# Two layers of a hybrid diffusion backbone on one core: another order at an FFN edge, at the start and at the end of attention

## What is computed

```python
x = x + mod[2] * rms_norm(y, mix_post_g[l])
h = modulate(rms_norm(x, ffn_pre_g[l]), mod[3], mod[4])
x = x + mod[5] * rms_norm(conv_ffn(h, ffn_w_in[l], ffn_conv_w[l], ffn_w_out[l]), ffn_post_g[l])
```

## Time and profile before

| | us |
|---|---|
| runs of the kernel | 1669.77, 1673.02, 1673.84 (median 1673.02) |
| the profiled execution's own time | 1669.0 |
| its span | 1667.3 |
| busy in the span: PE, DVE, ACT, POOL | 1607.5, 1024.0, 551.7, 54.6 |
| chain that ended last: PE, DVE, ACT, issue, POOL | 77%, 14%, 3%, 2%, 1% |

### The profile page before, as it was taken

The page is one execution under the profiler, slowest core; times in us unless marked ns, Lnnn a source line. Parts: engine busy times, 40 slices in busy tenths (PEclk is TensorE's granted clock), DMA queues, the critical chain, the costliest instruction groups (busy, mean ns, idle before and its releaser), DMA issues.

```text
span 1667.3 us, 21933 instructions
## 1 busy us (share of the span) xinstructions
PE 1607.5 (96%) x8698; PEld 1347.4 (81%) x8698; DVE 1024.0 (61%) x1457; ACT 551.7 (33%) x878; POOL 54.6 (3%) x74
## 2 busy tenths in 40 slices
PE   5999999999999999999999999898999999999998
PEld 2688887787898878888888887787778988888886
DVE  2899996659757774667626446654875644454344
ACT  3313224555633221123211225613325532232133
POOL 0500000210000000000000001100000000000001
PEclk9999999989999999999999999999999999999999
DMA  9421212334116552454323231230002233223222
GB/s 309 137 67 51 77 51 70 115 111 111 39 53 226 205 172 79 139 193 166 129 83 133 51 101 51 80 101 26 26 1 63 89 101 112 79 89 113 88 95 81
DMA packets 134009, 169.43 MB, mean 102 GB/s; under 512 B 15970, under 2 KB 92450, under 8 KB 133930
## 3 DMA queue, kind: packets, MB, share of 16 engines
q1 hardware_dynamic: 133360, 168.11, 31.5%
q10 hardware_dynamic: 570, 0.22, 0.1%
HBM read 166.17 MB, written 2.15 MB: 101 GB/s over the span
## 4 chain that ended last, share of the span: by engine, by line
PE 77%; DVE 14%; ACT 3%; issue 2%; POOL 1%; POOLq 0%; DVEq 0%; ACTq 0%
PE acc L700 39%; PE acc L755 21%; DVE conv_u L1845 7%; PE acc L726 4%; PE acc L912 2%; DVE w_lo L1570 2%; PE acc L1120 2%; PE acc L1099 2%; PE acc L813 1%; PE acc L947 1%; PE acc L1067 1%; PE acc L668 1%; DVE x L1745 1%; PE acc L925 1%; POOL y L2263 1%
## 5 line engine op out<-in xcount | busy, mean ns | idle before, releaser
L700 PE MATMUL acc<-h_hi,w_hi 128*128 128x512 f32 (+1 forms) x1424 | 414.1, 352 | 3.0 <-issue 2.4
L700 PE MATMUL acc<-h_lo,w_hi 128*128 128x512 f32 (+1 forms) x1424 | 411.1, 350 | 0.0
L700 PE MATMUL acc<-h_hi,w_lo 128*128 128x512 f32 (+1 forms) x1424 | 411.1, 350 | 0.0
L1570 DVE TENSOR_TENSOR w_lo<-raw,w_hi 128x1024 fp32r<-128x1024 f32 x183 | 219.6, 1229 | 155.6 <-ACT w_hi L1139 155.5
L700 PEld LDWEIGHTS acc<-h_hi,w_hi 128*128 128x128 f32 x1424 | 229.8, 188 | 40.6 <-issue 3.4
L1139 ACT ACTIVATE w_hi<-raw 128x1024 fp32r<-128x1024 f32 x183 | 186.5, 1055 | 225.8 <-PE acc L755 183.9
L700 PEld LDWEIGHTS acc<-h_lo,w_hi 128*128 128x128 f32 x1424 | 229.6, 188 | 37.4 <-issue 0.5
L700 PEld LDWEIGHTS acc<-h_hi,w_lo 128*128 128x128 f32 x1424 | 229.4, 188 | 37.2
L755 PE MATMUL acc<-w_hi,hid_hi 128*128 128x512 f32 x440 | 176.3, 401 | 0.0
L755 PE MATMUL acc<-w_lo,hid_hi 128*128 128x512 f32 x440 | 175.6, 399 | 0.0
L755 PE MATMUL acc<-w_hi,hid_lo 128*128 128x512 f32 x440 | 175.5, 399 | 0.0
(11 more groups left out here) (245 smaller groups left out, 2051.7 us busy)
## 6 DMA issues: line engine op xcount, KB each, us to landing
ada_w<-in_ada_w SPq DMA_DIRECT2D x88, 512.0 KB, 5.9
raw<-in_ffn_w_in SPq DMA_DIRECT2D x88, 512.0 KB, 3.6
raw<-in_ffn_w_out SPq DMA_DIRECT2D x44, 512.0 KB, 4.2
raw<-in_even_w_in SPq DMA_DIRECT2D x24, 512.0 KB, 4.5
ada<-in_ada_w SPq DMA_DIRECT2D x8, 1024.0 KB, 12.2
raw<-in_odd_w_in SPq DMA_DIRECT2D x12, 512.0 KB, 4.2
raw<-in_even_w_out SPq DMA_DIRECT2D x8, 512.0 KB, 4.5
ada_m<-in_ada_w SPq DMA_DIRECT2D x8, 512.0 KB, 4.4
```

The costliest lines, as they stand in the source:

```text
L700: last = nc.tensor.matmul(acc[:, s, m, t0:t1], w[:, slot, kk, c], x_[:, k, t0:t1], start=(k == 0 and q == 0), stop=(k == KD - 1 and q == 2))
L1570: return nc.vector.tensor_tensor(out_, in0, in1, op)
```

## The change

- **FFN edges.** POOL's part goes. DVE gates columns 512 to 1023 itself, into the scratch `ada_d`, between the sum of a tile and the wait for its root, and adds in two halves (`added`). At down02 the additions, squares and normalisations of tiles 4 and 5 come after all steps of the latent tiles and after the last granule's high and low parts. PE turns tiles 4 and 5 one after the other, after the third of the four first blocks. In every edge ACT does one Sqrt on a constant before it waits for the first half.
- **First scores.** The row sums for the keys move from behind value tile 4 to behind tile 3, score 0 from after the values to behind tile 4. ACT copies value tiles 0 to 3 when they are done, then does one Exp on a constant; tiles 4 and 5 it copies after the exponential of round 0.
- **First granule of out1.** `PAIRS` makes heads 0 and 1 its first granule, then heads 2 and 3, the pool, heads 4 and 5. Its banks change sides (near and far). The inner `step` of `token_products` becomes a function of its own, `token_step`, unchanged. Rounds 22 and 23, which have no scores to make ahead, each make two tiles of granule 0. DVE's low parts of rounds 2 and 3 move behind the loop. The first unit of the second FFN waits for the set that holds the other half of out1.

```diff
+PAIRS = {"out0": (2, 0, 1, 3), "out1": (1, 2, 0, 3)}
...
@@ tile_bank
             near, far = U[name] % 2, 1 - U[name] % 2
+            if name == "out1":
+                near, far = far, near
...
@@ token_products
-            if not freed:
+            if not freed and not begun:
                 psum_free(pe, d)
...
-                for g in range(half):
+                for g in range(1 if begun and not a else 0, half):
...
@@ ffn of PE
                         else:
+                            if l:
+                                psum_free(pe, U["up10"] + 1)
                             first_products(pe, U[f"up{l}0"], G[f"up{l}0"], h, [(256 * e, 256 * e + 256) for e in range(nt // 2)],
...
@@ first_products of in1
-                           lambda e: turn(pe, "down02", NT - 2 + e) if e < 2 else None)
+                           lambda e: [turn(pe, "down02", j) for j in (NT - 2, NT - 1)] if e == 2 else None)
...
@@ values on PE
+                if j == 3:
+                    last.then_inc(sem("v_tiles"), 1)
...
-                if j == 4:
+                if j == 3:
                     pe.wait_ge(sem("pool_taken"), 1)
                     pe.wait_ge(sem("rot_taken"), 4)
                     pe.wait_ge(sem("kdiag_ready"), 2)
...
                     last.then_inc(sem("kb_full"), 1)
+                if j == 4:
+                    pe.wait_ge(sem("v_taken"), 1)
+                    pe.wait_ge(sem("qk_ready"), 1)
+                    scores(0)
 
             u = U["att"]
             psum_free(pe, u + 1)
-            pe.wait_ge(sem("qk_ready"), 1)
...
-            scores(0)
             scores(1)
...
@@ attention rounds on PE
                 if n + 2 < N_Q * NL:
                     scores(n + 2)
+                else:
+                    pe.wait_ge(low, G["out1"] + 5)
+                    pe.wait_ge(h_ready, HEADS + 2)
+                    for j in (n % 2, n % 2 + 2):
+                        last = token_step(pe, "out1", h, 0, 0, j)
+                    if n == N_Q * NL - 1:
+                        last.then_inc(part_used, 1)
...
-            token_products(pe, "out1", h, lambda k: pe.wait_ge(h_ready, HEADS + k + 1))
+            token_products(pe, "out1", h, lambda k: pe.wait_ge(h_ready, HEADS + k - 1) if k >= 2 else pe.wait_ge(sem("pool_low"), 1),
+                           begun=True)
...
@@ edge of ACT
+                nc.scalar.activation(mark[:, 5:6], eps[:, 0:1], ACT.Sqrt)
                 act.wait_ge(y_eps, EDGES.index(name) + 1)
...
-                    act.wait_ge(x_new, q + 1)
-                    x_squares(j, NT + q, junk_x[:, :])
+                    if name != "down02" or j < NL:
+                        act.wait_ge(x_new, q + 1)
+                        x_squares(j, NT + q, junk_x[:, :])
...
                     take_high(n + 2 * half + 3)
+                    if name == "down02":
+                        for j in range(NL, NT):
+                            act.wait_ge(x_new, t.chain + j + 1)
+                            x_squares(j, NT + t.chain + j, junk_x[:, :])
...
@@ values on ACT
-            psum_full(act, u)
-            nc.scalar.activation(v1[:, 0:4, :], acc[:, u % 2, 0, :].rearrange("p (j c) -> p j c", c=256), ACT.Copy)
-            nc.scalar.activation(v1[:, 4:6, :], acc[:, u % 2, 1, 0:512].rearrange("p (j c) -> p j c", c=256), ACT.Copy
-                                 ).then_inc(set_free[u % 2], 1)
+            act.wait_ge(sem("v_tiles"), 1)
+            nc.scalar.activation(v1[:, 0:4, :], acc[:, u % 2, 0, :].rearrange("p (j c) -> p j c", c=256), ACT.Copy
+                                 ).then_inc(sem("v_taken"), 1)
+            nc.scalar.activation(mark[:, 6:7], eps[:, 0:1], ACT.Exp)
...
                 if n == 0:
+                    psum_full(act, u)
+                    nc.scalar.activation(v1[:, 4:6, :], acc[:, u % 2, 1, 0:512].rearrange("p (j c) -> p j c", c=256), ACT.Copy
+                                         ).then_inc(set_free[u % 2], 1)
                     unit_high(G["vin"] + 4)
...
@@ edge of DVE
+                def added(j):
+                    q = t.chain + j
+                    if not mixer:
+                        tile_taken(dve, name, 1, j)
+                        dve.wait_ge(x_new, q)
+                        sd.done(vt(ada_d[:, :], y[:, j, 512:1024], gates[idx][:, stream(j), 512:1024], ALU.mult))
+                    dve.wait_ge(y_root, q + 1)
+                    sd.done(nc.vector.reciprocal(yroot[:, 1, j:j + 1], yroot[:, 0, j:j + 1]))
+                    sd.wait()
...
+                    for half_, of in ((0, y[:, j, 0:512]), (1, ada_d[:, :])):
+                        x_ = x[:, j, 512 * half_:512 * half_ + 512]
+                        ins = nc.vector.scalar_tensor_tensor(x_, of, yroot[:, 1, j:j + 1], x_, ALU.mult, ALU.add)
+                    ins.then_inc(x_new, 1)
...
                     summed(name, 2, 1, j)
+                    if 1 <= j <= NL:
+                        normed(j - 1)
+                    if j >= 3:
+                        tile_low(name, j - 3)
+                    if j < NL:
+                        added(j)
+                    if j >= 2:
+                        tile_half(name, j - 2, l, comp)
...
                 if not mixer:
+                    tile_low(name, NL - 1)
+                    take_low(n + 2 * half + 3)
+                    for j in range(NL, nt):
+                        added(j)
                     nc.vector.memset(poolw[:, :, :], 0.0).then_inc(sem("poolw_zero"), 1)
-                    normed(nt - 1)
-                    tile_low(name, nt - 3)
-                take_low(n + 2 * half + 3)
+                    for j in range(NL, nt):
+                        normed(j)
...
@@ attention on DVE
-                if n == 2:
-                    unit_low(G["in1"] + 14)
-                elif n == 3:
-                    dve.wait_ge(sem("pool_high"), 1)
-                    vt(h_lo[:, 0:2, 0:LAT], ps2[:, :, 0:LAT], h_hi[:, 0:2, 0:LAT].bitcast(F32), ALU.subtract).then_inc(h_ready, 2)
...
+            dve.wait_ge(sem("pool_high"), 1)
+            vt(h_lo[:, 0:2, 0:LAT], ps2[:, :, 0:LAT], h_hi[:, 0:2, 0:LAT].bitcast(F32), ALU.subtract).then_inc(sem("pool_low"), 1)
+            unit_low(G["vin"] + 4)
             head_low(N_Q - 1)
...
@@ POOL: edge("down02") and edge("down12") removed
```

More of the change, by code:

```diff
@@ L741, in turn, with token_step, token_products @@
             last.then_inc(turned, 1)
-        def token_products(pe, name, lhs, ready, freed=None, amid=None):
+        def token_step(pe, name, lhs, a, g, j):
+            half, m_ = TOK[name].half, G[name] + a * TOK[name].half + g
+            for kk in range(2):
+                k = 2 * pair_of(name, g) + kk
+                for q, (w, x_) in enumerate(((w_hi, lhs[0]), (w_lo, lhs[0]), (w_hi, lhs[1]))):
+                    last = nc.tensor.matmul(tile_bank(name, a, j), x_[:, k, j * P:(j + 1) * P],
+                                            w[:, m_ % 4, 2 * kk:2 * kk + 2, :].rearrange("p a c -> p (a c)"),
+                                            start=(g == 0 and kk == 0 and q == 0), stop=(g == half - 1 and kk == 1 and q == 2))
+            return last
+        def token_products(pe, name, lhs, ready, freed=None, amid=None, begun=False):
             t, d, n = TOK[name], U[name], G[name]
             nt, half = t.nt, t.half
-            def step(a, g, j):
-                m_ = n + a * half + g
-                for kk in range(2):
-                    k = 2 * pair_of(name, g) + kk
-                    for q, (w, x_) in enumerate(((w_hi, lhs[0]), (w_lo, lhs[0]), (w_hi, lhs[1]))):
-                        last = nc.tensor.matmul(tile_bank(name, a, j), x_[:, k, j * P:(j + 1) * P],
-                                                w[:, m_ % 4, 2 * kk:2 * kk + 2, :].rearrange("p a c -> p (a c)"),
-                                                start=(g == 0 and kk == 0 and q == 0), stop=(g == half - 1 and kk == 1 and q == 2))
-                return last
-            if not freed:
+            if not freed and not begun:
                 psum_free(pe, d)
@@ L796, in token_products @@
                             pe.wait_ge(cols_taken, list(BESIDE).index(name) + 1)
-                        last = step(a, g, j)
+                        last = token_step(pe, name, lhs, a, g, j)
                         if g == half - 1:
@@ L1054, in _, with scores @@
             product(pe, U["kin"], G["kin"], h, always, amid=heads_45)
+            def scores(n):
+                hd, i = divmod(n, NL)
+                if n >= 2:
+                    pe.wait_ge(sem("score_exp"), n - 1)
+                for t0, t1 in SEGS[T]:
+                    last = nc.tensor.matmul(acc[:, 0, n % 2, t0:t1], inb[:, 2 + hd, i * P:(i + 1) * P],
+                                            kT[:, hd // 3, t0:t1], start=True, stop=True)
+                last.then_inc(sem("score_full"), 1)
             u, n = U["vin"], G["vin"]
@@ L1088, in _ @@
                     last.then_inc(sem("kb_full"), 1)
```

(22 more changed lines are left out.)

44 lines of the change are left out of this document (18 added, 26 removed).

## The result

The changed kernel takes 1657.41 us (median of 4 runs, 1656.99 to 1659.79). The kernel before, on the same chip, takes 1671.39 us (4 runs, 1669.67 to 1673.84). The ratio is 0.9918 with a 95% interval of 0.9904 to 0.9932: 14.0 us faster. The profiled execution of the changed kernel took 1657.77 us, its span is 1656.1 us against 1667.3 before, 11.2 us less.

What follows compares the result with a forecast made beforehand. TensorE, busy 96% of the span, bounds the kernel, so only its idle and half-clock time can be won. The terms sum to -11.35 us on 1669.0, so 1657.6; for the median, 4.0 above, 1661.6, range 1655 to 1667.

Steps and rivals of the forecast that it cites:

- rival without new cold stretches: Third unit and up10: the new waits leave the clock at full speed, 3.4 us more won, 1658.2 us; chance 0.2.
- Term 1: Edge of down02: third unit starts 4.0 us earlier, less 1.7 for a cold clock: -2.3 us.
- Term 2: Attention's start: first softmax hidden under value tile 5, rounds of 3.31 us from the start: -7.5 us.
- Term 3: Rounds 22 and 23: out1's first granule fills them, 9.7 us instead of 14.1: -4.2 us.
- Term 4: up10's first unit waits for out1's last sum: 1.7 us lost, 1.7 more for a cold clock: +3.4 us.
- Term 5: Tail, down12: the last x no longer waits 0.85 us for GpSimd, less 0.1 for the split: -0.75 us.
- The table load: Before each root: rival with ScalarE idle 1.4 us beyond the load, a drain, 1660.2 us; chance 0.03.

Runs made afterwards that it cites:

- e9: The changed kernel, nothing edited, profiled a second time: span 1656.6 us against 1656.1 in the first profile.
- e4: Changed kernel with the six tiles of down02 back in their old order, context tiles not last: 1659.23 us, ratio 0.9939 to the kernel before.
- e1: Kernel before with only the FFN edge's part of the change: 1668.45 us, ratio 0.9987.
- e7: Changed kernel with the squares and sum of out1's last tile ahead of two granules of up10: 1656.41 us, ratio 0.9910 to the kernel before.
- e2: Kernel before with only the first scores' part of the change, low parts left in rounds 2 and 3: 1666.61 us, ratio 0.9972.
- e3: Kernel before with only the part for out1's first granule, low parts moved behind the loop: 1667.41 us, ratio 0.9981.
- e5: Changed kernel without the Sqrt ahead of the edges and the Exp ahead of attention: 1662.19 us, ratio 0.9951 to the kernel before.
- e11: Changed kernel with out1's last squares and sum first, nothing further edited, profiled a second time: span 1654.4 us against 1654.9.
- e10: Changed kernel with down02's tiles in their old order, nothing further edited, profiled a second time: span 1656.5 us against 1657.4.

## Why the prediction was right

The direction and the places held, and 1657.4 lies in the range, 4.2 us below the predicted 1661.6. It is nearest to the rival without new cold stretches, 1658.2, but by luck: the third unit's stretch was there, so that rival's condition failed. Of the difference, 1.6 us are the base: I added the changes to a median of 1673.0, and the kernel before took 1671.4 beside the changed one. 2.6 us remain between the 11.35 predicted and the 14.0 of the medians. The stages explain 1.4 of them in the first profile (12.7 us in all) and none in e9 (9.7), so how near the number came is in part luck too. By the prediction's own steps:

**Term 1, edge of down02 (-2.3, measured -1.93).** Each link of the series came as listed: third unit at 1076.08, or 1074.6 less the executions' offset of 1.5 us, against 1075.0; one wait of 4.19 us against 4.5; both context tiles turned from 1064.23, or 1062.7, against 1063.0. What was mis-sized is the cold stretch: 12 matmuls at 0.43 us pitch instead of 0.23 cost 2.4 us, not 1.7. Whose merit the term is, the prediction didn't part; e4 does: VectorE's gating with the Sqrt ahead brings 2.9 us, and the new order of the tiles costs 1.0. e4's stage holds a half-clock stretch of its own behind the last granule's wait, 1.7 us of TensorE's time; with both kernels' stretches taken out, A would be 63.7 with the new order and 63.4 with the old one, an estimate, so the order would win nothing even then. The prediction also says that "its cold stretch goes too" behind the shortened first wait. It was gone in the changed kernel's two profiles, but not in those of e1 and e7, with the same wait of 1.9 us; A lost nothing by it there: 65.26, or 63.6 without the third unit's stretch, as in the changed kernel.

**Term 2, first scores (-7.5, measured -7.32).** Score 0 starts at 1150.81 with no wait. Predicted was 1151.1 on the clock of before; the key multiplication ends at 1150.18, 0.6 us ahead (0.4 was said). The value copy costs 0.69 us and pT 0.22, against 0.6 and 0.45. e2 shows what the term hid: with the low parts left in rounds 2 and 3 it was -3.1, or some -4.8 without e2's half-clock stretch. In e9, the same kernel, B is 85.13: this term is then -5.8, by the half-clock stretch behind the head sums.

**Term 3, granule amid the rounds (-4.2, measured -4.50).** Rounds of 4.74 us against 4.85; no wait for granules 4 to 7 of out1. e3 alone gives -4.51. The prediction's own figures (14.1 less 9.7) make -4.4, not the -4.2 that it wrote.

**Term 4, its price (+3.4, measured +1.86 in one profile, +3.36 in the other).** The wait is 2.91 us for exactly the sum named, against 3.1. The 1.7 us for a cold clock came in e9 and not in the first profile. The prediction priced a cold stretch as a rule (behind 3 us or more always, behind less never); the runs show a chance. Full speed came behind 3.10 us in e2 and behind 3.19 and 3.32 us in e3, half clock behind 1.86 us in e7. That is the step that failed, here and in the rival "no new cold stretches", which treats the third unit and up10 as one case: the third unit was cold each time, up10 in three profiles of seven, and amid the values it was cold without a wait. The rival also misread the kernel before: its 4.52 us wait is followed by full speed for three matmuls, but the granted clock is 0.62 over the 4.5 us behind it, so all three of its waits of over 3 us had gone cold. The listed times of term 1 take the gain of that stretch in without naming it.

**Term 5, tail (-0.75, measured -0.64 in G and -0.19 in F).** The last tile's root is now waited for directly, and the wait for GpSimd has given way to a shorter one for ACT. Changed kernel, DVE's last rows:

```profile
1651.40 0.16 DVE L1763 RECIPROCAL small<-small 128x1 f32<-128x1 f32 x1 [0.39 <-ACT small L1247]
1651.60 0.75 DVE L1771 SCALAR_TENSOR_TENSOR x<-y,small,x 128x512 f32<-128x512 f32 x1
1652.27 0.75 DVE L1771 SCALAR_TENSOR_TENSOR x<-ada_d,small,x 128x512 f32<-128x512 f32 x1
```

**The table load.** ACT's timeline of the changed kernel at the new Exp shows a load as long as in the earlier trace rows and its operation 0.02 us behind it:

```profile
1146.61 1.28 ACT L1554 ACT_TABLE_LOAD   x1
1147.91 0.20 ACT L1554 ACTIVATE small<-small 128x1 f32<-128x1 f32 x1
```

The Trainium skill (ScalarE: Activation LUTs, What ACT_TABLE_LOAD costs) adds a drain of some 1.38 us to a switch. e5 puts the load back on the chain, and the first turning comes 1.2 us later: the load's length, without a drain. Here the measurement differs from the page, and decides.

**What stays open.** The trace differs by 11.2 us (10.7 in e9), the medians by 14.0. Both kernels' profiled executions are within their runs; the profiled one of before is 2.4 us below its median, that of the changed kernel 0.4 above. More half-clock stretches in the runs of before don't explain it: the mean granted clock is 0.9884 over the 39 runs of before that have one on record and 0.9896 over five of the changed kernel, 2.0 us apart by that, and the two profiled executions differ by more (0.989 and 0.991). The cause of the missing 2.8 us stays open.

## What to carry to other kernels

When steps are put last to let others go first, look at what already stood behind them: here two small copies, one high and one low part held the next unit as long as the new order had won. Moving them ahead was worth 6 us by the stages; the order alone was worth nothing. A resource that two products hand over (the swapped banks) costs what stands ahead of the last reader in that reader's queue, so put that read first. And a single profile tells a difference of 1.5 us from a clock stretch only by the granted clock of the stretch; subtract it, or take a second profile, before a cause is named.

## What the runs showed of the hardware

- The same kernel, profiled twice, has half-clock stretches in different places. Behind the 2.9 us wait at up10 the granted clock was 1.00 in one profile and 0.76 over 6 us in the next; amid the values, with PE busy 20.00 of 20 us, 1.00 in one and 0.92 in the next (e9), and the reverse for e7 (0.93) and e11 (1.00). The two profiles of e4 and of e7's kernel come from different chips; on one chip the runs of e1 had mean clocks from 0.985 to 0.992.
- The longer the wait, the more often the clock was at a half behind it: 2 of 9 at 1.9 us, 4 of 11 at 2.2 to 2.7, 3 of 7 at 2.9, 6 of 9 at 3.1 to 3.3, 8 of 8 above 4 us. It could fall a matmul or three after the wait (e10: 0.39 us for the first, then 0.57 over 4 us).
- Amid the values the stretch, where there was one, began 0.1 to 1.2 us behind 24 matmuls of one column each (six profiles of 13), with no wait.
- A table load costs ACT 1.28 us in each of these profiles, and where nothing else held the next operation it starts 0.01 to 0.02 us after it.
